# The MLP of a decoder trunk over 1024 tokens by one level of a seven-product matrix scheme

## What is computed

```python
def conv_gated_ffn(h, w_up, conv_w, conv_b, w_down):
    gate, val = jnp.split(h @ w_up, 2, axis=-1)      # w_up: 1024 x 5632
    gate = causal_dwconv(gate, conv_w, conv_b)       # width 3
    return (jax.nn.silu(gate) * val) @ w_down        # w_down: 2816 x 1024
x = x + g2 * conv_gated_ffn(h, ff_up, ff_conv_w, ff_conv_b, ff_down)
return rmsnorm(x, final_g)
```

## Time and profile before

| | |
|---|---|
| median of 3 runs | 3033.74 us (3032.5 to 3036.54) |
| span of the profiled execution, first to last instruction | 3029.5 us |
| the median less that span | 4.2 us |
| TensorE busy with matmuls | 95% of the span |
| VectorE, ScalarE, GpSimd busy | 61%, 36%, 45% |
| DMA | 329 MB, 109 GB/s |
| granted TensorE clock, mean | 0.997 |

### The profile page before, as it was taken

How to read it: one execution, slowest core, us unless ns; L and a number is a source line. 1 busy time by engine, 2 the same in 40 slices (tenths; PEclk the granted TensorE clock), 3 DMA queues, 4 the chain that set the end, 5 groups by cost and what they waited for, 6 DMA issues and landing times.

```text
span 3029.5 us, 42819 instructions
## 1 busy us (share of the span) xinstructions
PE 2892.4 (95%) x13303; PEld 2366.1 (78%) x13303; DVE 1846.2 (61%) x2844; ACT 1082.4 (36%) x1734; POOL 1377.8 (45%) x960
## 2 busy tenths in 40 slices
PE   1889999999999999999998999999999999999998
PEld 1568888888877888888887788888887788888886
DVE  4685846565377774565628685565546778365653
ACT  0343333343334333343324433343333443243432
POOL 0543444555444344555444334455554434455553
PEclk9999999999999999999999999999999999999999
DMA  8343222334243322333334232233434332233332
GB/s 314 108 129 112 80 91 80 100 93 142 91 141 101 112 77 77 101 92 101 132 116 140 84 101 86 82 93 100 132 98 127 126 101 77 87 87 100 93 136 101
DMA packets 201303, 329.04 MB, mean 109 GB/s; under 512 B 18389, under 2 KB 110009, under 8 KB 197051
## 3 DMA queue, kind: packets, MB, share of 16 engines
q1 hardware_dynamic: 197394, 324.09, 33.9%
q10 hardware_dynamic: 3754, 2.96, 0.3%
HBM read 318.46 MB, written 8.53 MB: 108 GB/s over the span
## 4 chain that ended last, share of the span: by engine, by line
PE 84%; issue 7%; DVE 5%; ACTq 1%; POOL 1%; DMA 1%; ACT 0%; DVEq 0%; POOLq 0%
PE main L981 73%; PE main L1008 2%; PE pair L1084 2%; DVE acc L699 1%; POOL w_lo L354 1%; PE pair L1069 1%; PE pair L934 1%; DVE arow L744 1%; PE pair L1109 1%; PE pair L1076 1%; ACTq L380 1%; DMA small<-in_ssd_dt_bias_dram 1%; PE pair L1022 0%; PE pair L1120 0%; PE pair L1131 0%
## 5 line engine op out<-in xcount | busy, mean ns | idle before, releaser
L354 POOL TENSOR_TENSOR w_lo<-w_raw,w_hi 128x512 fp32r<-128x512 f32 x944 | 1353.4, 1444 | 1551.8 <-ACT w_hi L396 1050.9
L396 ACT ACTIVATE w_hi<-w_raw 128x512 fp32r<-128x512 f32 x595 | 371.3, 630 | 1002.6 <-PE main L981 756.8
L981 PE MATMUL main<-h_hi,w_hi 128*128 128x512 f32 x1776 | 695.2, 391 | 12.8 <-POOL w_lo L354 12.3
L981 PE MATMUL main<-h_lo,w_hi 128*128 128x512 f32 x1776 | 691.4, 389 | 0.0
L981 PE MATMUL main<-h_hi,w_lo 128*128 128x512 f32 x1776 | 691.3, 389 | 0.0
L981 PEld LDWEIGHTS main<-h_hi,w_hi 128*128 128x128 f32 x1776 | 333.4, 188 | 90.1 <-POOL w_lo L354 19.1
L981 PEld LDWEIGHTS main<-h_hi,w_lo 128*128 128x128 f32 x1776 | 333.4, 188 | 69.6
L981 PEld LDWEIGHTS main<-h_lo,w_hi 128*128 128x128 f32 x1776 | 333.5, 188 | 68.1
L515 ACT ACTIVATE w_hi<-w_raw 128x512 fp32r<-128x512 f32 x352 | 216.8, 628 | 394.9 <-PE main L981 394.9
L981 PE MATMUL main<-w_hi,h_hi 128*128 128x512 f32 x768 | 319.0, 415 | 0.0
L981 PE MATMUL main<-w_hi,h_lo 128*128 128x512 f32 x768 | 300.3, 391 | 0.0
(11 more groups left out here) (199 smaller groups left out, 4081.9 us busy)
## 6 DMA issues: line engine op xcount, KB each, us to landing
w_raw<-in_ff_up_dram SPq DMA_DIRECT2D x352, 256.0 KB, 3.1
w_raw<-in_w_in_dram SPq DMA_DIRECT2D x292, 256.0 KB, 2.8
w_raw<-in_ff_down_dram SPq DMA_DIRECT2D x176, 256.0 KB, 2.7
w_raw<-in_w_out_dram SPq DMA_DIRECT2D x128, 256.0 KB, 2.6
ada_t<-in_ada_w_dram SPq DMA_DIRECT2D x24, 1024.0 KB, 13.6
arow<-acs_scratch SPq DMA_DIRECT2D x16, 1024.0 KB, 4.8
x<-in_x_dram SPq DMA_DIRECT2D x4, 2048.0 KB, 8.0
xn<-in_x_dram SPq DMA_DIRECT2D x16, 512.0 KB, 8.0
```

The lines of the kernel that those rows point to most:

```text
L354: nc.gpsimd.tensor_tensor(w_lo[:, s, :], w_raw[:, s, :], w_hi[:, s, :].bitcast(F32), ALU.subtract).then_inc(w_lo_ok, 1)
L396: nc.scalar.activation(w_hi[:, n % RING, :], w_raw[:, n % RING, :], ACT.Copy).then_inc(w_hi_ok, 1)
L981: ins = T.matmul(main[i][:], a, w, start=first and p == 0, stop=last and p == 2)
```

## The change

Two blocks are taken together for the MLP, 1024 tokens. Each of its two products is cut in halves in tokens, in the summed dimension and in the output's columns, and computed by seven products of half size in place of eight (P1, P2, P6, P7, P4, P5, P3), with sums of quarters of the left operand (S1 to S4) and of the weight (T1 to T4), and sums of the products. The parts:

- The order of the work is mixer(0), mixer(1), MLP(0), mixer(2), mixer(3), MLP(1), all written out with no loops.
- The up-projection is 77 products (11 column groups by 7) of two units each, in a rotation of four pairs of PSUM banks (`UP_SET`). The down-projection is 77 units, 11 for each of seven products, which use `main` and `aux` in turn. One unit of weights at the end is loaded and split and not multiplied.
- T1 to T4 of both weights are made in mixers 0 and 1: for each of 33 tiles SP loads four 256 KB quarters, GpSimd does four subtractions or additions of 128x512 (`t_step`), SP stores four tiles to DRAM scratch (`t_store`). Tile by tile that happens every four units, from unit 4 to unit 78 in mixer 0 (18 tiles) and from unit 14 to 78 in mixer 1 (15 tiles). MLP units read the sums from there.
- The normalised residual of an even block is transposed and scaled in the next mixer (`raw_transpose`, `raw_tiles`), stored (`h2_d`) and read back (2 MB, at unit 100 of the odd mixer) as `raw0`. That of an odd block is transposed between up products 2 and 3 and the next. VectorE makes S3, S2, S4, S1 and the low parts of seven operands.
- The next even block's input is normalised and transposed in the down-projection, an odd block's in OUT of the mixer before.
- VectorE adds every product from PSUM into `c_gate` and `c_val` (`collect`); the convolution works on two tiles at once, ScalarE does its first tap (`taps`); the gated result g goes to DRAM in 11 stores of 1 MB (`store_g`) and comes back in 15 pieces (11 MB, `load_g`). Its halves' sums and hi and lo parts are made unit by unit in the down-projection (`sums`, `low`, `a_high`).
- The residual of both blocks goes through DRAM (`store_x2`). The last norm works on whole halves: `free_half0`, `finish(s, 1)`, `finish(s, 0)`. For the first pair these are in VectorE's program of mixer 2: the first two behind `da_t` and ahead of the first convolution, the third behind the second group's convolutions. Their buffers lie on `stage`, so ScalarE waits for `y0_free` before it moves the first group there. SP's stores wait for them at units 14 and 22 of mixer 2. For the last pair they come at the end.
- The 22 matmuls of L1170 and the split form of the first unit go.

The core of the diff:

```diff
+    P1, P2, P6, P7, P4, P5, P3 = range(7)
+    KH, QN, KG = KD // 2, KF // 2, KF // 2
+    assert QN == KG == 11 and KH == 4
+    UP_ORDER = [(0, P1), (0, P2), (1, P1), (1, P2)]
+    UP_ORDER += [(q, p) for q in (0, 1) for p in (P6, P7, P4, P5, P3)]
+    UP_ORDER += [(q, p) for q in range(2, QN) for p in range(7)]
+    NUP = len(UP_ORDER)
...
+    UP_SET = [2, 3, 0, 1, 0, 1] + [(2, 3, 0, 1)[n % 4] for n in range(NUP - 6)]
+    DOWN = 2 * NUP
+    ND = 7 * KG
+    FU = DOWN + ND + 1
...
+            def t_load(t):
+                sp.wait_ge(t_st[t % 2], 64 * (t // 2))
+                for which in range(4):
+                    dst = tb[t % 2][which][:]
+                    if t < 2 * QN:
+                        sp.dma_start(k_pair(dst), up_quarter(which, t // 2, t % 2)).then_inc(t_ld[t % 2], 16)
+                    else:
+                        sp.dma_start(dst, down_quarter(which, t - 2 * QN)).then_inc(t_ld[t % 2], 16)
+            def t_store(t):
+                sp.wait_ge(t_add, 4 * t + 4)
+                for which, holds in enumerate((T2, T4, T3, T1)):
+                    dst = tu_d[t // 2, holds, t % 2] if t < 2 * QN else td_d[holds, t - 2 * QN]
+                    sp.dma_start(dst, tb[t % 2][which][:]).then_inc(t_st[t % 2], 16)
+            def store_x2(b):
...
+                if b == 2 and n == 14:
+                    store_y(0, 1)
+                if b == 2 and n == 22:
+                    store_y(0, 0)
+                if b < 2:
+                    at, of = T_AT[b], T_OF[b]
+                    for t in of:
+                        if n == at + 4 * (t - of[0]):
+                            if b == 1 and t == of[0]:
+                                sp.wait_ge(x2_st, 16)
+                            t_load(t)
+                        if n == at + 4 * (t - of[0]) + 6:
+                            t_store(t)
+                if n == OUT + 12:
...
+                        if b % 2 and n == MU - 4:
+                            sp.wait_ge(w_used, mix0(b) + OUT + 3 * KD + RING)
+                            sp.wait_ge(h2_st, 16 * (b // 2 + 1))
+                            sp.dma_start(raw0[:].rearrange("p k t -> p (k t)"), h2_d[:]).then_inc(h2_ld, 16)
...
+                    if j == 7:
+                        sp.wait_ge(w_used, f0 + DOWN + RING)
+                        load_g(range(4, 10))
+                    if j == 10:
+                        store_g(s, QN - 1)
+                    if j == 12:
+                        sp.wait_ge(g_st, 32 * (s * QN + QN))
+                        load_g(range(10, len(G_PIECES)))
...
+            def t_step(t, step):
+                b11, b21, b12, b22 = (tile[:] for tile in tb[t % 2])
+                if step == 0:
+                    pool.wait_ge(t_ld[t % 2], 64 * (t // 2 + 1))
+                else:
+                    pool.wait_ge(t_add, 4 * t + step)
+                dst, one, other, how = ((b12, b22, b12, ALU.subtract), (b11, b12, b11, ALU.add),
+                                        (b21, b11, b21, ALU.subtract), (b22, b22, b11, ALU.subtract))[step]
+                nc.gpsimd.tensor_tensor(dst, one, other, how).then_inc(t_add, 1)
+            for b in range(2):
+                for n in range(MU):
+                    low(mix0(b) + n)
+                    for t in T_OF[b]:
+                        step = n - (T_AT[b] + 4 * (t - T_OF[b][0]) - 2)
+                        if 0 <= step < 4:
+                            t_step(t, step)
...
+                if b == 2:
+                    free_half0(0)
+                    finish(0, 1)
...
+                    if n == 1:
+                        for kk in range(2):
+                            s3(kk)
+                        for kk in range(2):
+                            s2(kk)
+                        for kk in range(2):
+                            s4(kk)
+                            op_low(s, P6, s2_raw, (kk,))
+                    if n == 3:
+                        op_low(s, P7, a11, range(2))
+                        for kk in range(2):
+                            s1(kk)
+                        op_low(s, P4, a22, range(2))
+                        dve.wait_ge(sum_ok, s * 8 + 8)
...
+                def sums(p, k):
+                    if p == P6:
+                        g_here(3, k)
+                        dve.wait_ge(s3_ok, s * KG + k + 1)
+                        if k >= 3:
+                            dve.wait_ge(a_lo_ok, s * ND + P6 * KG + k - 2)
+                        V.tensor_tensor(s_tmp[:, k % 3, :], g22[:, k, :], g11[:, k, :], ALU.subtract).then_inc(s2_ok, 1)
+                        dve.wait_ge(s2_ok, s * KG + k + 1)
+                        V.tensor_tensor(g12[:, k, :], g12[:, k, :], s_tmp[:, k % 3, :], ALU.subtract).then_inc(s4_ok, 1)
+                    elif p == P2:
+                        g_here(2, k)
+                        V.tensor_tensor(g11[:, k, :], g11[:, k, :], g21[:, k, :], ALU.subtract).then_inc(s3_ok, 1)
+                    elif p == P7:
+                        V.tensor_tensor(g21[:, k, :], g21[:, k, :], g22[:, k, :], ALU.add).then_inc(s1_ok, 1)
...
+            def free_half0(s):
+                dve.wait_ge(d_add, s * 14 + 14)
+                gate_y2(s, 0, 1)
+                add_y(s, 0, 1)
+            def finish(s, half):
+                if half:
+                    dve.wait_ge(pool_fin, s * 4 + 4)
+                    add_y(s, 1, 0)
+                    add_y(s, 1, 1)
+                for t in range(NT):
+                    if half:
+                        half_stats(1, 0, t)
+                    last = half_stats(half, 1, t)
+                link(last)
+                for t in range(NT):
+                    link(V.bn_aggr(mv[:, t, :], fstats[:, half, t, :, :]))
                 rms_rstd(NT)
+                dve.wait_ge(fin2_in, 32 * (s + 1))
                 for t in range(NT):
-                    V.scalar_tensor_tensor(out=x2[:, t, :], in0=x2[:, t, :], scalar=rstd[:, t:t + 1], in1=fg_bc[:],
-                                           op0=ALU.mult, op1=ALU.mult).then_inc(out_ok, 1)
+                    V.scalar_tensor_tensor(out=x_half[half][:, t, :], in0=x_half[half][:, t, :], scalar=rstd[:, t:t + 1],
+                                           in1=fg_bc[:], op0=ALU.mult, op1=ALU.mult).then_inc(y2_ok, 1)
+            for b in range(NB):
+                mixer(b)
...
-                for i in range(22):
-                    T.matmul(aux[3], h_hi[:, 0, 0:P], h_hi[:, 0, :], start=True, stop=True)
-                pe.wait_ge(xn_ok, b * (NT + 2) + (NT + 1))
...
+                for n, (q, p) in enumerate(UP_ORDER):
+                    got = sets[UP_SET[n]]
+                    set_free(n)
+                    for kk in range(2):
+                        u = f0 + 2 * n + kk
+                        pe.wait_ge(w_lo_ok, u + 1 + RING)
+                        if q == 0:
+                            pe.wait_ge(op_lo_ok, s * 14 + 2 * p + kk + 1)
+                        hi = w_hi[:, u % RING, :].rearrange("p (k n) -> p k n", k=2)
+                        lo = w_lo[:, u % RING, :].rearrange("p (k n) -> p k n", k=2)
+                        for i in range(2):
+                            cols = slice(i * P, (i + 1) * P)
+                            for kl in range(2):
+                                k = 2 * kk + kl
+                                for m, (w, a) in enumerate(((hi, op_hi[p]), (hi, op_lo[p]), (lo, op_hi[p]))):
+                                    ins = T.matmul(got[:, i, :], w[:, kl, cols], a[:, k, :], start=k == 0 and m == 0,
+                                                   stop=k == KH - 1 and m == 2)
+                        ins.then_inc(w_used, 1)
+                    if n == 2:
+                        pe.wait_ge(c_cp, s * QN + 1)
+                        pe.wait_ge(c_add, s * 77 + 1)
+                        raw_transpose(b, range(4), aux)
+                    if n == 3:
+                        raw_transpose(b, range(4, KD), aux)
+                for j in range(ND):
...
+                    for i in range(NT):
+                        ts = slice(i * P, (i + 1) * P)
+                        for m, (a, w) in enumerate(((hi, w_hi), (hi, w_lo), (lo, w_hi))):
+                            ins = T.matmul(banks[i], a[:, ts], w[:, u % RING, :], start=k == 0 and m == 0,
+                                           stop=k == KG - 1 and m == 2)
...
```

904 lines of the change are left out of this document (657 added, 247 removed).

## The result

The changed kernel takes 3065.55 us (median of 4, 3056.37 to 3068.15), the kernel before 3033.12 (4 runs, 3031.35 to 3036.54): a ratio of 1.0103, 95% interval 1.0089 to 1.0116. It is 1.0% slower; I had forecast 2991 us, with a range up to 3055. The profiled run took 3067.55 us, its span 3065.8.

What follows compares the result with a forecast made beforehand. TensorE's number of matmuls, 0.2267 us each, was taken as the bound. A gain of 216 us less added costs of 173 left 43 less: span 2986.5, median 2991 us, range 2915 to 3055, the forecast's own 2955 to 3027.

Steps and rivals of the forecast that it cites:

- weight sums in mixers 0, 1: Mixers 0 and 1: 132 added GpSimd instructions slow VectorE, costing 46 us (bounds 0 to 137); their DMA is hidden.
- start of up: Start of the up-projection: VectorE's sums and low parts delay P6 and P4, 7 us per pair, 14 (0 to 30).
- up to down: Between up- and down-projection: VectorE's last collection, gate and first low part cost 6 us per pair, 12 (8 to 20).
- down: Down-projection: g transfers 5 us, P6 3 per pair, next block's norm in P5 3; sum 14 (4 to 40).
- the end: After the last matmul: the final norm on whole halves takes 40 us against 13 before, +27 (20 to 32).
- unrolling: Loop ends: writing the loops out gains nothing, as the up-projection's window shows no fetch stall on TensorE.
- The gain of 216: TensorE: 792 MLP matmuls less give 179.5 us, 88 unused ones 20.0, waits inside the MLP 16.5; together 216.
- port rival: Mixers 0 and 1: VectorE and GpSimd block each other at full price, 137 for 46, 3082 us; with other slower ends 0.19.
- Mixer 2: Mixer 2: the first pair's finish delays convolutions by 25 us and SP's unit 22 by 18; sum 44 (10 to 65).
- The clock: Matmuls behind stalls run at 1.2 GHz, 0.2267 us more each, 27 us or less; put in the range.
- Absorbed stalls: Ring and slack hide half the weight sums, mixer 2's SP stop and half its delay: 2938 us, chance 0.21.
- rival of no change: DMA queues or GpSimd's waits take the 43 us, 40 in the down-projection, 17 in mixers: 3034 us; within 0.2%, chance 0.07.

Runs made afterwards that it cites:

- e10: Changed kernel without any weight sums, both their transfers and GpSimd's 132 instructions left out, products reading plain quarters: 2955.64 us, ratio 0.9747.
- e4: The kernel before with all its loops written out and nothing else changed: 3027.94 us, ratio 0.9985.
- e1: Changed kernel with GpSimd's 132 weight-sum instructions left out, the transfers kept: 2984.05 us, ratio 0.9835.
- e2: Changed kernel with GpSimd's 132 instructions kept, but only 4 of 33 weight-sum tiles loaded and none stored: 3054.91 us, ratio 1.0065.
- e6: Changed kernel, all work kept, the next block's norm, transposes and low parts in P5 reordered in pairs of tiles: 3051.69 us, ratio 1.0066.
- e3: Changed kernel without the first pair's last norm and stores in mixer 2, and without the waits for them: 3029.84 us, ratio 0.9990.
- e5: Changed kernel, all work kept, only the order of the first pair's finish in mixer 2 changed: 3035.12 us, ratio 1.0008.
- e7: Changed kernel, all work kept, 18 weight-sum tiles moved within mixers 0 and 1 and 15 into the first up-projection: 3007.24 us, ratio 0.9924.

## Why the prediction was wrong

Two terms were too small, the weight sums above all (46 in place of 110) and the down-projection (14 in place of 39); the others held within a few us. Stage times of the changed kernel, less the matmuls and transposes in each, against the terms:

| term | forecast | measured |
|---|---|---|
| weight sums in mixers 0, 1 | 46 | 110 (e10) |
| odd mixers, `raw_tiles` | 4 | about 0 |
| `raw0` behind the last tiles | 9 | 6.5 (5.2 and 1.3) |
| start of up | 14 | 15 (7.0 and 8.0) |
| up to down | 12 | 16 |
| down | 14 | 39 |
| start of mixer 2 | 3 | 6 |
| finish in mixer 2 | 44 | 40 |
| the end | 27 | 26 |
| unrolling | 0 | -5 (e4) |

The right column sums to 254 against 173, and against the 216 that goes it leaves 38 more; the spans differ by 3065.8 - 3029.5 = 36.3. That it closes so well is in part chance: 3.9 of the 36.3 lie ahead of the first unit (119.9 us against 116.0), and the profiled runs of the experiments, with the same work there, range from 116.2 to 119.5.

**The gain of 216 was right.** 880 matmuls went, a steady product is 5.44 us. (4 x 4.2 is 16.8 and not 16.5, which moves nothing.)

**"Weight sums in mixers 0 and 1" failed, 46 in place of 110.** The mechanism was the one I named, VectorE slowed by GpSimd, and I had its price at 0.9 us per instruction that matters. What I had wrong is how many matter. In UV I took the average slack of the stage (33 of 129 us) and charged 5 per block. Against e10 it cost 21 and 23 us, and more than half of that in UV 0 alone (44.6 against 31.2 in both), where VectorE is busy for 42.5 us in place of 30.6 and its chain begins with those 16 short operations: 11.48 us with the sums, 6.31 in e1, 7.37 in e10. In z I charged near 10 per block and it was 21 and 20, since VectorE is the chain there for the whole 60 us. In xbc I had 11 and 5, it was 15 and 9.

The transfers I had called hidden, by their bytes. Without the instructions beside them they cost 28.4 us (e1 less e10): they stand in SyncE's queue ahead of weight tiles, with SyncE's waits between them, in e1 for the stores, in the changed kernel's program for GpSimd too. With the instructions they cost 10.6 (e2). So 11 to 28 of the 110 are theirs, and no run divides it further.

The port rival was to decide from 0.67 us per added instruction. It was 0.83 with the transfers, which that rival did not count, and for the instructions alone 0.62 (e1) to 0.75 (e2 less e10), on both sides of 0.67. So the runs lie between my term and the port rival's 137. That its 3082 is nearer to the 3065.55 than my 2991 owes something to luck: it charged nothing for the queue and too little for the down-projection.

The Trainium skill's rule (SBUF — State Buffer, SBUF: two separate sides) is borne out in kind by the rows: an operation of 0.16 us took 1.15 and ended with the GpSimd instruction beside it, and 16 short ones took 11.48 us. As a price of a whole instruction each, 170 to 190 us, it is too dear: 81.5 to 99.3 us went with the 132 instructions, since many fall where VectorE has room.

**"Down" failed, 14 in place of 39.** P1, P2 and P6 of the two pairs lost 11.0 and 10.4 us where I had 5.5 and 5.5. I had put 2.5 of each pair on the g transfers in P1. They run at a DMA share of 0.86 and 310 GB/s, above the 290 that I had taken as the full rate, and cost one pause of 1.6 us at the end of P1, where ScalarE waits 5.7 us for a weight tile. (By the prediction's own 44 and 43.5 us they would have cost 0.5; its 2.5 does not follow.) The other 2.8 of the 4.4 us that P1 of the first pair loses are the clock: behind the wait of 8 us on the way into it, 12 matmuls follow 0.43 us apart. P6 loses 4.7 where I had 3, and P2 1.9 where I had nothing. The rest is P5 of the first pair, 17.5 in place of 3. I counted the next block's norm as work for which VectorE has time, which it has; but it waits for ScalarE, ScalarE for TensorE's transposes, and the low part of TensorE's next unit stands behind that wait. e6 took 12 of the 17.5 away with all the work kept.

**"Mixer 2" held**: 40 against 44, 23.6 in the first two groups where I had 25 and 17.0 in the third where I had 18, and e3 and e5 show the cause as told. **"The end" held** to 1 us, **"start of up"** too.

**The clock** I gave at most 27 us, as a rival of its own. It is no case apart: TensorE's excess of some 64 us of busy time comes with the stalls. In UV 0 of block 0 TensorE is busy 32.1 us where the same work takes 26.9 in e10, in z 64.1 against 58.6; that is about a third of what these stages lost. I had 120 slow matmuls at 0.2267 us, there were 193 at 0.20, 39 us; I had put them in the range and not in the sum. How much of the 64 is also time of the run was not measured by itself.

**The other rivals.** Absorbed stalls (2938) fell with the weight sums; e7 and e5 show that 58 of the 110 and 30 of mixer 2's 40 can be absorbed, but by another order. The rival of no change had the right stage in part: the down-projection reached 39 of the 40 us that were its bound.

## What to carry to other kernels

Work given to an idle engine costs by where it stands and not by its sum: the same 33 tiles cost 110 us beside stages in which VectorE is the chain, and 52 when 15 of them lay in a stage with room for VectorE and the others away from the tightest groups (e7 against e10). Take slack from the first operations after a wait, not as an average over a stage, and count a queue's waits as well as its bytes. A scheme that removes matmuls wants the work around it placed anew; here three changes of order turned 1.0% slower into 2.2% faster, which is still less than a third of the 216 us removed. And add what the clock takes behind each stall: 0.20 us for each matmul at the lower level.
